# Sparse attention by per-head keys and values, with another layout of the on-chip memory

## The reference, cut to what matters

```python
q, c, qi, ki, wi = split(h @ w_in)           # q: 16 heads x 64, c: 128 latents, qi: 8 x 64, ki: 64
c = rms_norm(c, kv_norm_g)
q_lat = einsum('bshd,hdc->bshc', q, w_uk) * ATT_SCALE
dots = relu(einsum('bqhd,bsd->bqhs', qi, ki))
score = einsum('bqh,bqhs->bqs', wi, dots)    # causal; the 64 best keys are kept for each query
logits = einsum('bqhc,bqkc->bqhk', q_lat, c_sel) + rel_bias[...]
p = softmax(logits)
o_lat = einsum('bqhk,bqkc->bqhc', p, c_sel)
o = einsum('bshc,hcv->bshv', o_lat, w_uv)
x = x + o @ w_o
```

## Time and profile before

| | |
|---|---|
| three runs | 913.70, 913.99, 916.32 us; median 913.99 |
| the profiled execution | 915.44 us, its span 913.7 us |
| mean granted clock of TensorE | 0.994 |
| busy: TensorE, VectorE, ScalarE, GpSimd | 900.9, 582.8, 466.6, 65.1 us |
| chain of waits that ended last | TensorE 91%, VectorE 3%, ScalarE 2%, GpSimd 2% |
| moved by transfers | 163.94 MB, 179 GB/s in the mean |

### The profile page before, as it was taken

One profiled execution on the slowest core, in us unless ns is written; L12 is line 12 of the kernel. 1 busy time (PEld: TensorE's weight loads), 2 busy tenths in 40 slices (PEclk: granted clock), 3 DMA queues, 4 the chain that ended last, 5 costly groups with the idle time before them and its releaser, 6 DMA issues.

```text
span 913.7 us, 14878 instructions
## 1 busy us (share of the span) xinstructions
PE 900.9 (99%) x5988; PEld 797.4 (87%) x5988; DVE 582.8 (64%) x968; ACT 466.6 (51%) x752; POOL 65.1 (7%) x97
## 2 busy tenths in 40 slices
PE   8999999999999999999999999999999999999998
PEld 5998799999997996678999999887898889999996
DVE  5769665555554596646556565563568788888764
ACT  5686454444443565635445454444457674443550
POOL 0010000000000017600000000030100000000000
PEclk9999999999999998999999999999999999999999
DMA  8525885555545844328636555540524455554541
GB/s 316 233 93 184 303 309 188 186 188 187 184 141 182 324 141 147 130 69 329 231 139 248 190 175 189 184 150 1 185 99 136 152 203 184 185 177 146 176 147 46
DMA packets 28582, 163.94 MB, mean 179 GB/s; under 512 B 3169, under 2 KB 7649, under 8 KB 10210
## 3 DMA queue, kind: packets, MB, share of 16 engines
q1 hardware_dynamic: 28514, 162.99, 50.2%
HBM read 161.93 MB, written 1.05 MB: 178 GB/s over the span
## 4 chain that ended last, share of the span: by engine, by line
PE 91%; DVE 3%; ACT 2%; POOL 2%; issue 1%; DMA 1%; DVEq 0%; POOLq 0%; ACTq 0%
PE ps L272 15%; PE ps L273 15%; PE ps L274 15%; PE ps L285 11%; PE ps L287 11%; PE ps L286 11%; DVE WL L1521 2%; PE ps L410 2%; PE ps L880 1%; PE ps L881 1%; PE ps L879 1%; PE ps L350 1%; PE ps L794 1%; POOL LG L2353 1%; PE ps L819 1%
## 5 line engine op out<-in xcount | busy, mean ns | idle before, releaser
L1521 DVE TENSOR_TENSOR WL<-RAW,WH 128x1024 fp32r<-128x1024 f32 (+1 forms) x264 | 313.2, 1224 | 114.2 <-ACT WH L957 113.8
L272 PE MATMUL ps<-XAh,WH 128*128 128x256 f32 x1152 | 330.2, 287 | 2.0 <-ACT WH L957 1.8
L273 PE MATMUL ps<-XAl,WH 128*128 128x256 f32 x1152 | 326.5, 283 | 0.0
L274 PE MATMUL ps<-XAh,WL 128*128 128x256 f32 x1152 | 326.5, 283 | 0.0
L957 ACT CAST WH<-RAW 128x1024 fp32r<-128x1024 f32 (+1 forms) x264 | 261.1, 1041 | 73.4 <-PE ps L287 64.9
L272 PEld LDWEIGHTS ps<-XAh,WH 128*128 128x128 f32 x1152 | 221.3, 192 | 11.3 <-issue 7.0
L273 PEld LDWEIGHTS ps<-XAl,WH 128*128 128x128 f32 x1152 | 221.4, 192 | 1.6 <-issue 0.2
L274 PEld LDWEIGHTS ps<-XAh,WL 128*128 128x128 f32 x1152 | 221.5, 192 | 0.0
L287 PE MATMUL ps<-WH,HTl 128*128 128x512 f32 x256 | 101.1, 395 | 0.0
L286 PE MATMUL ps<-WL,HTh 128*128 128x512 f32 x256 | 100.9, 394 | 0.0
L285 PE MATMUL ps<-WH,HTh 128*128 128x512 f32 x256 | 100.9, 394 | 0.0
(11 more groups left out here) (254 smaller groups left out, 1138.0 us busy)
## 6 DMA issues: line engine op xcount, KB each, us to landing
RAW<-in_w_dram SPq DMA_DIRECT2D x141, 1024.0 KB, 4.9
RI<-in_w_dram SPq DMA_DIRECT2D x2, 1024.0 KB, 10.1
GB<-in_gb_dram SPq DMA_DIRECT2D x4, 512.0 KB, 7.1
BI<-in_dbias_dram SPq DMA_DIRECT2D x16, 128.0 KB, 3.9
NB<-in_nbias_dram SPq DMA_DIRECT2D x16, 128.0 KB, 2.0
RAW<-in_w_dram SPq DMA_DIRECT2D x2, 528.0 KB, 3.5
X<-in_x_dram SPq DMA_DIRECT2D x4, 256.0 KB, 3.4
RAW<-in_w_dram SPq DMA_DIRECT2D x2, 512.0 KB, 6.6
```

What stands on the lines that cost most here:

```text
L272: T.e.matmul(dst, h, xh[:, k, :], start=k == 0, stop=False)
L273: T.e.matmul(dst, h, xl[:, k, :], start=False, stop=False)
L274: last = T.e.matmul(dst, l, xh[:, k, :], start=False, stop=k == 7)
L1521: D.e.tensor_tensor(M.WL[:, c.s, sl], M.RAW[:, c.r, sl], M.WH[:, c.s, sl].bitcast(F32), ALU.subtract).then_inc(*S.lo.tick(key, a))
```

## The change

- **Keys and values per head.** The key weights `UK` are transposed once (`key_weights`) and multiplied by the latents to 16 heads' keys `KD` (`keys`); the latents are multiplied by `UV` to 16 heads' values `VD` (`values_of`). `latent`, `qlev`, `oev` and `outs` go. The queries are scaled by 0.125 as they are evicted.
- **Heads in pairs.** `logits(m)` makes both heads of a pair in banks 4 and 5: the mask by a matmul with the identity (`IDR`), then the products of queries and keys, 64 rows for each head. VectorE then adds only the bias, which the queue brings in two transfers in the layout of the logits (`BI`, 384 columns). GpSimd's `biased` goes. `values(m)` writes both heads' outputs to 64 rows each of bank 7.
- **Order.** The products of keys and values stand between the indexer's products and the queries; chunk `q` 3 and the groups of `wo` 0 and 1 stand inside the loop. `UK` and `UV` are transferred ahead of chunk `up` 8 of the first MLP. `WL` of `q` 2 and `q` 3 is made by GpSimd.
- **Layout.** `WH`, `WL`, `XA`, `XB` and the arena come first, and `RAW`, `X`, the constants, statistics, `GB`, `XN` and small tiles lie above them.
- **Outset.** Three matmuls of zeros stand between the transposes of the input and the first chunk.

```diff
@@ class Memory
-        self.RAW = self.tile("RAW", [128, NRAW, 2048])
         self.WH = self.tile("WH", [128, NW, 2048], F32R)
         self.WL = self.tile("WL", [128, NW, 2048], F32R)
-        self.X = self.tile("X", [128, 2, 1024])
         self.XA = ...
...
+        self.top = self.highest
+        self.RAW = self.tile("RAW", [128, NRAW, 2048])
+        self.X = self.tile("X", [128, 2, 1024])
+        self.CP = self.tile("CP", [128, self.C["end"]])
...
@@ tensor_rec
     for t in range(2):
         first_transposes(T, M, S, t)
+    for i in range(3):
+        made = T.e.matmul(M.PS[5][:, :], M.AR[:, 0, 0:128], M.AR[:, 0, :], start=True, stop=True)
+    made.then_inc(*S.warm.tick())
@@ tensor_dsa
+    def key_weights(n):
+        T.wait_ge(S.uk, 16)
+        T.wait_ge(*S.kiev.at(n))
+        for q in range(4):
+            at = n * 512 + q * 128
+            made = T.e.transpose(M.PS[6 + n][:, q * 128:(q + 1) * 128], M.UK[:, at:at + 128], M.cc("id", 0, 128))
+    def keys(i):
+        for m in range(2):
+            at = (2 * i + m) * 128
+            made = T.e.matmul(M.PS[bank][:, m * 256:(m + 1) * 256], M.UKT[:, at:at + 128], M.CT[:, 0:256], start=True, stop=True)
+    def values_of(t, n):
+        T.e.matmul(M.PS[(6, 1)[t] + n][:, :], M.CT[:, t * 128:(t + 1) * 128], M.UV[:, n * 512:(n + 1) * 512], ...)
...
     def logits(m):
+        T.wait_ge(*S.qev.at(m // 2))
+        T.wait_ge(*S.kdev.at(m // 2))
+        for h2 in range(2):
+            T.wait_ge(*(S.ttr.at(2 * m - 2 + h2, 1) if m else (S.kdev.at(3), S.rlh.at(7))[h2]))
+        for t in range(2):
+            T.wait_ge(*S.mask.at(t))
+        T.wait_ge(*S.idr.at())
+        for h2 in range(2):
+            T.e.matmul(M.PS[4 + h2][:, 0:384], M.IDR[:, :], M.MS[:, :], start=True, stop=False)
+        for a0, a1, q0 in ((0, 128, 0), (128, 384, 128)):
+            for h2 in range(2):
+                hp = 64 * h2
+                made = T.e.matmul(M.PS[4 + h2][:, a0:a1], M.QT[hp:hp + 64, m, q0:q0 + 128], M.KD[hp:hp + 64, m, 0:a1 - a0], start=False, stop=q0 > 0)
...
     def values(m):
+        T.wait_ge(*S.pev.at(2 * m + 1))
+        for t, c0 in ((0, 0), (1, 128)):
+            for h2 in range(2):
+                h = 2 * m + h2
+                made = T.e.matmul(M.PS[7][64 * h2:64 * h2 + 64, at + c0:at + 256], M.VD[:, t, h * 64:(h + 1) * 64],
+                                  M.PT[:, h % 4, 256 * t:256 * t + 256 - c0], start=t == 0, stop=t == 1)
...
+    dots(0); key_weights(0); dots(1); key_weights(1); dots(2); keys(0); dots(3); keys(1); keys(2); keys(3)
+    values_of(1, 0); values_of(1, 1); values_of(0, 0); values_of(0, 1)
+    queries(0, whole); queries(1, whole); queries(2, whole[:2])
+    logits(0); queries(2, whole[2:3]); logits(1); queries(2, whole[3:])
+    for p in range(1, 11):
+        if p < 9:
+            turn(2 * p - 2)
+        if p < 5:
+            queries(3, whole[p - 1:p])
+        if 5 <= p < 9:
+            wo((p - 5) // 2, int(p % 2 == 0), 0)
+        if p < 9:
+            turn(2 * p - 1)
+        if p < 7:
+            logits(p + 1)
+        if 5 <= p < 9:
+            made = wo((p - 5) // 2, int(p % 2 == 0), 1)
...
+        if p >= 2 and p < 10:
+            values(p - 2)
@@ vector_dsa: scores, and the loop of pairs
+    for h in range(8):
+        score(h)
+        if h in (5, 6):
+            low(D, M, S, "q", 0, halves=(h - 5,))
...
+    for p in range(11):
+        if p >= 8 and p % 2 == 0:
+            out_low(p // 2 - 2)
+        if p < 8:
+            logits(2 * p)
+            logits(2 * p + 1)
+            inverse_sums(2 * p)
+            if p in (4, 6):
+                out_low(p // 2 - 2)
+            if p:
+                low(D, M, S, "wo", (p - 1) // 2, halves=((p - 1) % 2,))
+            inverse_sums(2 * p + 1)
@@ pool_program
-            P.e.tensor_tensor(M.BM[:, h % 2, a0:a1], M.BI[:, h % 4, 256 - (a1 - a0):256], M.MS[:, a0:a1], ALU.add)...
+    low_by_pool("q", 2)
+    low_by_pool("q", 3)
@@ sync_program
     def bias(h):
         if h >= 4:
-            for t in range(2):
-                Y.wait_ge(*S.bm.at(h - 4, t))
-        Y.e.dma_start(M.BI[:, h % 4, :], D["dbias"][h]).then_inc(S.bi[h % 4], 16)
+            Y.wait_ge(*S.ttr.at(h - 4, 1))
+        Y.e.dma_start(M.BI[:, h % 4, 0:128], D["dbias"][h, :, 128:256]).then_inc(S.bi[h % 4], 16)
+        Y.e.dma_start(M.BI[:, h % 4, 128:384], D["dbias"][h]).then_inc(S.bi[h % 4], 16)
...
+        if key == ("up", 0, 8):
+            Y.wait_ge(*S.freed.at("wout", 3))
+            Y.e.dma_start(M.UK[:, :], D["uk"]).then_inc(S.uk, 16)
+            Y.e.dma_start(M.UV[:, :], D["uv"]).then_inc(S.uv, 16)
...
```

More of the change, by code:

```diff
@@ L376, in tensor_rec @@
     for i in range(2):
-        made = T.e.matmul(M.PS[5][:, :], M.AR[:, 0, 0:128], M.AR[:, 0, :], start=True, stop=True)
-    made.then_inc(*S.warm.tick())
+        T.e.matmul(M.PS[5][:, :], M.AR[:, 0, 0:128], M.AR[:, 0, :], start=True, stop=True)
     T.wait_ge(S.ident, 16)
@@ new lines, in keys @@
+    def keys(i):
+        bank = (6, 7, 0, 4)[i]
+        T.wait_ge(*S.uktev.at(i // 2))
+        T.wait_ge(*(S.uktev.at(i) if i < 2 else S.rlh.at(3)))
+        for m in range(2):
+            at = (2 * i + m) * 128
+            made = T.e.matmul(M.PS[bank][:, m * 256:(m + 1) * 256], M.UKT[:, at:at + 128], M.CT[:, 0:256], start=True, stop=True)
+        made.then_inc(*S.kd.tick(i))
+    def values_of(t, n):
+        T.wait_ge(S.uv, 16)
+        T.wait_ge(*(S.rlh.at(4 + n) if t else S.kdev.at(n)))
+        T.e.matmul(M.PS[(6, 1)[t] + n][:, :], M.CT[:, t * 128:(t + 1) * 128], M.UV[:, n * 512:(n + 1) * 512], start=True, stop=True).then_inc(*S.vd.tick(t, n))
@@ L656, in oready @@
+        made.then_inc(*S.pv.tick(m))
     def oready(j):
@@ L1198, in scalar_dsa @@
         A.e.copy(M.CT[:, t * 128:(t + 1) * 128], M.PS[6 + t][:, 128:256]).then_inc(*S.kiev.tick(t))
-    high(A, M, S, "q", 0)
-    for h in range(4):
-        rlh(h)
+    rlh(0)
+    rlh(1)
+    key_weights(0)
     evict(S.qiev, M.QI, 1, 2, "qi", 1)
-    high(A, M, S, "q", 1)
+    rlh(2)
+    key_weights(1)
+    rlh(3)
+    high(A, M, S, "q", 0, halves=(0,))
+    rlh(4)
+    keys(0)
+    rlh(5)
+    high(A, M, S, "q", 0, halves=(1,))
+    rlh(6)
+    keys(1)
+    rlh(7)
+    high(A, M, S, "q", 1)
@@ L1204, in scalar_dsa @@
+    keys(2)
+    keys(3)
+    values(1, 0)
+    values(1, 1)
+    values(0, 0)
+    values(0, 1)
     high(A, M, S, "q", 2)
     A.e.activation(M.stat("table"), M.NH[:, 0:1], AF.Exp)
-    for h in range(4, 8):
-        rlh(h)
-        if h == 5:
-            evict(S.qev, M.QT, 0, 1, "q", 0)
+    queries(0, 3)
     high(A, M, S, "q", 3)
-    def qlev(m):
-        A.wait_ge(*S.ql.at(m))
-        for h, b in ((2 * m, 0), (2 * m + 1, 3)):
-            if h >= 3:
-                A.wait_ge(*S.lg.at(h - 3))
-            A.e.activation(M.QL[:, h % 3, :], M.PS[b][:, 0:256], AF.Copy, scale=0.125).then_inc(*S.qlev.tick(h))
@@ L1232, in oth @@
[L1232 to L1243 removed]
+    queries(1, 0)
     exps(0)
     exps(1)
[L1246 to L1256 removed]
@@ L1257, in scalar_dsa @@
-    oth(3)
+    high(A, M, S, "wo", 0)
+    queries(2, 1)
+    for p in range(1, 11):
+        if p == 5:
+            queries(3, 2)
+        if p >= 8 and p % 2 == 0:
+            oth(p // 2 - 2)
+        if p < 8:
+            exps(2 * p)
+        if p in (4, 6):
+            oth(p // 2 - 2)
+        if p < 9:
+            pev(2 * p - 2)
+        if p < 8:
+            exps(2 * p + 1)
+        if p < 9:
+            pev(2 * p - 1)
+        if p < 7:
+            high(A, M, S, "wo", 1 + (p - 1) // 2, halves=((p - 1) % 2,))
@@ L1839, in vector_dsa @@
     scales(D, M, S)
-    low(D, M, S, "q", 0)
     def score(h):
@@ L2503, in sync_program, with __init__, of, at @@
     Y.wait_ge(S.out, 16 * outs)
+class Lows:
+    def __init__(self, vector, pool):
+        self.vector, self.pool = vector, pool
+    def of(self, key):
+        return self.pool if key in self.pool.place else self.vector
+    def at(self, *key):
+        return self.of(key).at(*key)
+    def tick(self, *key):
+        return self.of(key).tick(*key)
 def signals(nc, stack, M):
@@ L2529, in signals @@
     split = [(key, a) for key in M.SPLIT for a in range(2)]
-    S.hi, S.lo = count("hi", split), count("lo", split)
+    S.hi = count("hi", split)
+    by_pool = [(key, a) for key, a in split if key in (("q", 2), ("q", 3))]
+    S.lo = Lows(count("lo", [k for k in split if k not in by_pool]), count("lo_pool", by_pool))
     S.freed = count("freed", M.SPLIT)
@@ L2574, in signals @@
     S.qev = then(S.qiev, blocks)
-    S.qlev, S.pev, S.oev = (count(n, heads) for n in ("qlev", "pev", "oev"))
+    S.uktev, S.kdev, S.vdev = count("uktev", range(2)), count("kdev", blocks), count("vdev", [(1, 0), (1, 1), (0, 0), (0, 1)])
+    S.pev, S.idr = count("pev", heads), count("idr", one)
     S.ex, S.oth = count("ex", [(h, t) for h in heads for t in range(2)]), count("oth", blocks)
@@ L2639, in signals @@
     S.pn = count("pn", [(h, t) for h in heads for t in range(2)])
```

(1 more changed line is left out.)

321 lines of the change are left out of this document (130 added, 191 removed).

## The result

The changed kernel takes **898.5 us** (median of four runs, 897.22 to 899.77), the kernel before beside it 913.95. The ratio is 0.9825, with a 95% interval of 0.9804 to 0.9847: 15.5 us are gone. Predicted were 896.9, in a range of 891 to 904. The profiled execution has a span of 895.4 us (897.22 with what lies around it).

What follows compares the result with a forecast made beforehand. TensorE, busy 900.9 of 913.7 us, was taken as the bound. Attention -12, tile place -3.9 and -0.25, outset -0.9 sum to -17.1 us: 915.44 to 898.3, less 1.45 to the median, 896.9; range 891 to 904.

Steps and rivals of the forecast that it cites:

- A pair of heads: Attention loop: TensorE's work per pair falls from 4.84 to 3.0 us, saving 14.7 us over eight pairs.
- Work, net: Attention: 14.7 us saved on pairs, less 8.3 added once for key-weight transposes, keys and values: -6.4 us.
- Stalls: Attention loop, 337 to 398 us: TensorE's 3.0 us idle and 3.7 us of lost clock both go, -6.7 us.
- The clock's term: Attention loop: granted clock 0.94 on average over 61 us, counted as 3.7 us lost and recovered.
- the cover: Attention loop: q3's quarters and wo groups between pairs give TensorE 1.4 or 2.7 us more per phase, hiding other engines' work.
- Waits of TensorE: Sign of being right: no wait of TensorE above 0.5 us between 314 and 396 us.
- they are wanted in phase 4: Bias transfers of heads 8 to 11 queue behind wo3's, which waits for wo0's subtraction in phase 2; needed in phase 4.
- GpSimd's subtractions: q2 and q3: four subtractions of 2.1 us each, ready before wanted; by the skill's rule 0.5 us higher sum.
- The place of the tiles: Up projections: HT at low addresses saves 0.0051 us on each of 768 matmuls, -3.9 us; MT half of 0.5.
- Rival E: Fast class needs held and moving tiles apart, which the all-low layout breaks; columns' matmuls slow down: 918.7 us, chance 0.05.
- Rival D: Place does more: chunks multiplied by columns also gain, 0.0013 us on each of 3456 matmuls: 892.4 us, chance 0.10.
- The outset: Kernel start: three zero products keep the clock full, -1.7 us, but start the first chunk 0.8 later: -0.9 us.

Runs made afterwards that it cites:

- the bare loop: Changed kernel with q3's quarters moved ahead of the loop over head pairs and the parts of wo 0 and 1 behind it: 910.78 us, ratio 0.9953.
- the run with 192 bytes: Changed kernel with XA, XB and YA begun 192 bytes further on (modulo 256), no instruction changed: 885.86 us, ratio 0.9674 to the kernel before.

## Why the prediction was right, step by step

- **A pair of heads**: predicted 3.0 us, measured 2.72 (turns 0.55, mask 0.52, queries by keys 0.85, values 0.80). Right in kind; 8 x 0.28 = 2.2 us more gained than counted. The products carried over from other lines to within 0.07 us (0.85 for 0.79, 0.80 for 0.87). The mask didn't (0.52 for 0.36), nor did the transposes (0.55 for 0.81), and the 0.2 added for changes of kind isn't there on top: that these leave only 0.28 is in part luck.
- **Work, net**: predicted -6.4. At full clock the stage goes from 93.66 to 81.36, of which the idle time takes 4.1 - 0.6 = 3.5; the rest, 8.8, is work, and the pairs' 2.2 explain the difference.
- **Stalls**: predicted -6.7 (3.0 idle and 3.7 clock). The idle time in the typical execution was 4.1 and is 0.6, so -3.5. The clock's term was mis-sized twice: in the profiled execution the fall cost 1.5 us and not 0.06 x 61 = 3.7, and by their mean clock 38 of 54 executions don't have it. That the stalls would go was right, and it hung on the cover: in the bare loop 12.3 us come back.
- **Waits of TensorE**: none above 0.5 us between 314 and 396, as forecast; the largest of three is 0.2. The biases' queue, which I had traced ("they are wanted in phase 4"), is where VectorE loses 6.0 us, of which TensorE feels little: the attention stage is 0.8 shorter without them.
- **GpSimd's subtractions**: predicted 2.1 us each, measured 2.41 for three of them and 3.40 for the one that waited for VectorE. The Trainium skill (SBUF — State Buffer, Who interferes with whom) has a VectorE instruction with two SBUF inputs and a GpSimd instruction that reads SBUF exclude each other. The trace agrees: VectorE's subtraction ended 1.08 us after GpSimd's first and GpSimd's second 2.27 us after VectorE's, so that neither ran during the other. The loss was 0.9 us and not the whole 2.1 that I priced because VectorE came when 1.07 us of GpSimd's were left. It was hidden either way; the run with them on VectorE is no slower.
- **The place of the tiles**: -3.9 - 0.25 predicted, -4.3 measured alone, and the reason was wrong, so that the size came out is luck in part: the gap between the two classes was measured in rows, and the new layout happened to close it. (HT gave 3.6 and MT 0.5.) "What differs is the address" holds, "the fast class is low" doesn't: the beginning within 256 bytes, relative to the other operand, decides. MT, which I put "between the classes" at 130 KB, got the full -0.5; 146 KB and 157 KB with a whole-KB beginning are as fast as 8. Rival E's condition, held and moving "apart in some way", was nearer to the mechanism than my own. It didn't come true because the new layout gives all of them the same residue (beginning modulo 256 bytes).
- **YA**: I left it out of the sum. It lost what it had had by accident, 0.0013 x 96 = 0.12 us. Rival D read that 0.1187 as a gain of low places, when it was a gain of another residue; the run with 192 bytes shows that a gain is there, five times as large in the faster rhythm (0.0065) and 0.0022 for YA itself, which is in the slower one.
- **The outset**: predicted -0.9, and -0.87 is what the trace with the zeros alone has behind them. In the changed kernel it is -0.4 (the first weights were there 0.57 us later in that execution, 16.39 against 15.82), and by the median of twelve runs with the zeros alone -0.3, with an interval that holds zero. The step was right for the one execution; what it left out is that a later wait for `WL` takes part of the lead back and that some executions have no low clock there.
- **The sum**: -17.1 against -15.5 by the medians. It was near because the overvalued clock (3.7 for 1.5 or nothing) and the undervalued work (6.4 for 8.8) lie on opposite sides. There is a slip in its last step too: 3.7 for the fall was taken from the profiled execution, which had it, and then 1.45 more for that execution's distance from the median, although the distance is about what the fall costs. Without the second step the forecast is 898.3, against 898.5.

## What to carry to other kernels

Read a share of lost clock as a bound, not as time: the engine that ran slower had also waited less, and one execution's fall may be absent in most; look at several executions' mean clock before a term is made of it. When one stream of equal matmuls is 2% slower than another, compare where the two operands begin modulo 256 bytes before anything else; padding by 384 bytes gave 0.4%, and choosing the distance gave 1.4% more. When the steps of a loop are made shorter, count first what covers their waits: without the projections between the pairs, the shorter loop gave nothing (12.3 us came back).

## What was not expected of the hardware

- A matmul's time depends on (moving - held) modulo 256 bytes of the operands' beginnings in a partition: 0.2270 to 0.2333 us with 512 columns, 0.1133 to 0.1200 with 256 (4-byte numbers, full clock). The height in the partition, from 8 to 196 KB, changes nothing (0.2267 and 0.1200 throughout).
- With 256 columns and 192 bytes there are two rhythms, 0.1135 and 0.1178, each kept to the end of a stream of 48 to 143 matmuls once its first few are past.
- VectorE's instruction with one input tile (the mask, 128 columns) took 1.30 us beside GpSimd's subtraction and 0.22 without, and ended 0.08 us after it: it waited for GpSimd's to end, as the subtraction with two input tiles did. The maxima and replacements between them, with one input tile too, took 0.27 to 0.41 us beside GpSimd as without it.
